# Three places of a decoder-layer kernel reordered: opening loads, the last memory values against the first `w_co` tile, and a third row buffer for the output

## The reference

```python
mk_p, mv_p = memory_kv(mem_prompt, norm_mem, w_ck, w_cv)   # rmsnorm(256 memory rows) @ w_ck, @ w_cv
h = rmsnorm(x, norm_mix);  proj = h @ w_in                 # q|k|v|z_A|alpha|beta|u|z_B
# gated DeltaNet on q, k, v, and multi-scale pooling on u, both gated
x = x + concatenate([o_a, o_b]) @ w_out
qx = rmsnorm(x, norm_cross) @ w_cq                         # 4 heads of 512
probs = softmax(qx @ mem_k / sqrt(512))                    # prompt: 256 shared memory rows
ctx = probs @ mem_v                                        # each request: its own 256 cached rows
x = x + ctx @ w_co
y = rmsnorm(x, norm_final)
```

## Time and profile before

| | us |
|---|---|
| median of 3 runs | 1631.5 (1630.23 to 1631.87) |
| the profiled execution, its time | 1630.06 |
| the profiled execution, its span | 1628.2 |
| PE busy | 1603.5 |
| DVE busy | 1019.7 |
| ACT busy | 647.7 |

### The profile page before, as it was taken

How to read it: one execution, slowest core, us unless ns; L and a number is a source line. 1 busy time by engine, 2 the same in 40 slices (tenths; PEclk the granted TensorE clock), 3 DMA queues, 4 the chain that set the end, 5 groups by cost and what they waited for, 6 DMA issues and landing times.

```text
span 1628.2 us, 31254 instructions
## 1 busy us (share of the span) xinstructions
PE 1603.5 (98%) x12618; PEld 1486.8 (91%) x12618; DVE 1019.7 (63%) x1718; ACT 647.7 (40%) x1099; POOL 184.7 (11%) x191
## 2 busy tenths in 40 slices
PE   7999999999999999999999999999999999999997
PEld 5887899999999999999999999999999996499997
DVE  5676547775856767667344563443787754399952
ACT  5666344343452444425422232222344322235442
POOL 0121000211121111211100011111000000001120
PEclk9999999999999999999999999999999999999999
DMA  7898644233242432324289956878523359953462
GB/s 271 249 302 260 217 109 116 70 94 96 76 119 53 116 96 70 101 54 130 77 197 232 247 136 183 225 217 221 145 78 104 104 224 419 369 156 106 131 187 110
DMA packets 321886, 263.35 MB, mean 162 GB/s; under 512 B 15241, under 2 KB 288530, under 8 KB 316450
## 3 DMA queue, kind: packets, MB, share of 16 engines
q1 hardware_dynamic: 299360, 245.21, 50.8%
q10 hardware_dynamic: 22434, 16.87, 3.8%
HBM read 218.09 MB, written 44.30 MB: 161 GB/s over the span
## 4 chain that ended last, share of the span: by engine, by line
PE 94%; DVE 2%; DMA 1%; ACT 1%; issue 1%; POOL 0%; DVEq 0%; SPq 0%; ACTq 0%
PE pj L288 52%; PE pj L487 11%; PE pj L2318 7%; PE dk L2318 5%; PE pj L3091 2%; PE dk L2584 2%; PE pj L2617 1%; PE dk L1907 1%; PE pj L2595 1%; PE dk L1294 1%; PE pj L2626 1%; PE dk L371 1%; PE dk L1310 1%; PE dk L1410 1%; DMA values_raw_b<-in_cache_mem_v_dram 1%
## 5 line engine op out<-in xcount | busy, mean ns | idle before, releaser
L288 PE MATMUL pj<-a_hi,w_high 128*128 128x272 f32 x1792 | 392.1, 300 | 0.0
L288 PE MATMUL pj<-a_hi,w_low 128*128 128x272 f32 x1792 | 370.2, 288 | 0.0
L288 PE MATMUL pj<-a_lo,w_high 128*128 128x272 f32 x1792 | 369.4, 288 | 0.0
L288 PEld LDWEIGHTS pj<-a_hi,w_high 128*128 128x128 f32 x1792 | 280.3, 189 | 13.0 <-issue 7.7
L288 PEld LDWEIGHTS pj<-a_lo,w_high 128*128 128x128 f32 x1792 | 281.6, 188 | 0.0
L288 PEld LDWEIGHTS pj<-a_hi,w_low 128*128 128x128 f32 x1792 | 280.0, 189 | 0.0
L272 DVE TENSOR_TENSOR w_low<-w_raw,w_high 128x2048 fp32r<-128x2048 f32 x76 | 173.6, 2284 | 94.6 <-ACT w_high L262 94.4
L262 ACT ACTIVATE w_high<-w_raw 128x2048 fp32r<-128x2048 f32 x76 | 145.6, 1915 | 83.4 <-PE pj L288 46.1
L2202 ACT ACTIVATE q_high<-q_part 128x512 fp32r<-128x512 f32 x140 | 77.5, 621 | 74.1 <-DVE q_part L2256 36.0
L288 PE MATMUL pj<-mix_hi,w_high 128*128 128x272 f32 x512 | 105.9, 288 | 0.0
L288 PE MATMUL pj<-mix_lo,w_high 128*128 128x272 f32 x512 | 105.6, 288 | 0.0
(11 more groups left out here) (477 smaller groups left out, 2933.2 us busy)
## 6 DMA issues: line engine op xcount, KB each, us to landing
w_raw<-in_w_in_dram SPq DMA_DIRECT2D x48, 1024.0 KB, 6.0
w_raw_wide<-in_w_ck_dram SPq DMA_DIRECT2D x16, 1024.0 KB, 8.9
w_raw_wide<-in_w_cv_dram SPq DMA_DIRECT2D x16, 1024.0 KB, 6.2
w_raw<-in_w_out_dram SPq DMA_DIRECT2D x16, 1024.0 KB, 7.8
q_part<-in_w_cq_dram SPq DMA_DIRECT2D x48, 256.0 KB, 3.6
w_raw<-in_w_co_dram SPq DMA_DIRECT2D x8, 1024.0 KB, 7.2
q_part<-in_w_co_dram SPq DMA_DIRECT2D x32, 256.0 KB, 3.8
kin<-in_cache_mem_k_dram ACTq DMA_DIRECT2D x18, 256.0 KB, 6.2
```

The lines of the kernel that those rows point to most:

```text
L288: mm = pe.matmul(pj[:, 2 * (q % 2) + b, 0:n], wt[:, k, :], x(k, o, n), start=(k == 0 and m == 0), stop=(k == KT - 1 and m == 2))
```

## The change

It has three parts.

1. **Opening.** SP issues the first weight tile ahead of the second block of memory rows. ACT casts that tile before it takes the second block's squares, which now come behind `take_mem(0)`. DVE's `x_scale` of the second block comes behind the remainders of turn 0. On PE `turn_mem(1)` moves into `multiply_first`, behind the 8 matmuls of m = 0.
2. **Values.** The load of the first `w_co` tile goes behind both loads of request 7's values. On ACT the cast of that tile goes behind the copy of the requests' result (`svr`).
3. **End.** Block n = 4 gets a buffer of its own, `yb_short`, in the space of the weight ring, and waits for no store.

```diff
             sp.dma_start(cst[:, 0:NFIRST], ...).then_inc(const_loaded, 16)
-            sp.dma_start(xin[1][:], t["mem_prompt"][0, P:MEM, :]).then_inc(mem1_loaded, 16)
             for q in range(3):
                 sp.dma_start(raw_wide[q][:], source("mem", 0, q)).then_inc(w_loaded[q], 16)
                 if q == 0:
+                    sp.dma_start(xin[1][:], t["mem_prompt"][0, P:MEM, :]).then_inc(mem1_loaded, 16)
...
                         pe.matmul(pj[:, m, :], x[:, k, m * P:(m + 1) * P], high_wide[0][:, k, :], ...)
+                if m == 0:
+                    turn_mem_second(pe)
                 (second, third)[m](pe)
...
             turn_mem(0)(pe)
-            turn_mem(1)(pe)
...
-            x_stats(act, 1, xin[1], P)
+            cast_high(act, "mem", 0, 0)
             act.wait_ge(vec_ready, 1)
             take_mem(0)
-            cast_high(act, "mem", 0, 0)
+            x_stats(act, 1, xin[1], P)
             take_mem(1)
...
-            x_scale(dve, 1, xin[1], P)
             take_mem(0)
+            x_scale(dve, 1, xin[1], P)
             take_mem(1)
             split_low(dve, "mem", 0, 0)
...
             load_values(sp, 6)
-            sp.dma_start(raw[0][:], source("co", 0, 0)).then_inc(w_loaded[0], 16)
             sp.wait_ge(sv_done.sem, sv_done.at(3))
             load_values(sp, 7)
+            sp.dma_start(raw[0][:], source("co", 0, 0)).then_inc(w_loaded[0], 16)
...
-                    cast_high(act, "co", 0, 0)
                     act.wait_ge(sv_done.sem, sv_done.at(8))
                     act.activation(svr[:], pj[:, 0, :], ACT.Copy).then_inc(svr_a.sem, 1)
+                    cast_high(act, "co", 0, 0)
...
+        yb_short = put("yb_short", [D], F32, M_RAW)
+        def y_buffer(n):
+            return yb_short if n == 4 else yb[n % 2]
...
-                    at_least(act, y_stored[n % 2], 16 * (n // 2))
+                    at_least(act, y_stored[n % 2], 16 if n in (2, 3) else 0)
```

More of the change, by code:

```diff
@@ L493, in multiply_mem, with multiply_first @@
                         u += 1
-        def multiply_first(pe, second, third, fourth):
+        def multiply_first(pe, turn_mem_second, second, third, fourth):
             pe.wait_ge(hi_cast, 1)
@@ L572, in pe_mem @@
                     if j == 0 and q == 0:
-                        multiply_first(pe, turn_mem(2), turn_mem(3), turn_mem(4))
+                        multiply_first(pe, turn_mem(1), turn_mem(2), turn_mem(3), turn_mem(4))
                         continue
@@ L2897, in sp_co @@
                 dst = t["y_prompt"][0, n * P:(n + 1) * P, :] if n < 4 else t["y_sample"].rearrange("b t d -> (b t) d")
-                sp.dma_start(dst, yb[n % 2][0:rows, :]).then_inc(y_stored[n % 2], 16)
+                sp.dma_start(dst, y_buffer(n)[0:rows, :]).then_inc(y_stored[n % 2], 16)
             sp.wait_ge(y_stored[0], 48)
@@ L2936, in rows_out @@
                     act.wait_ge(y_turned.sem, y_turned_at(n, c))
-                    at_least(act, y_stored[n % 2], 16 * (n // 2))
-                    act.activation(yb[n % 2][0:rows, c * 512:(c + 1) * 512], y_bank(n, c)[0:rows, :], ACT.Copy,
+                    at_least(act, y_stored[n % 2], 16 if n in (2, 3) else 0)
+                    act.activation(y_buffer(n)[0:rows, c * 512:(c + 1) * 512], y_bank(n, c)[0:rows, :], ACT.Copy,
                                    scale=rs3[0:rows, n:n + 1]).then_inc(y_act, 1)
@@ L3025, in rows_out @@
                     dve.wait_ge(y_turned.sem, y_turned_at(n, c))
-                    at_least(dve, y_stored[n % 2], 16 * (n // 2))
-                    dve.tensor_scalar(yb[n % 2][0:rows, c * 512:(c + 1) * 512], y_bank(n, c)[0:rows, :], rs3[0:rows, n:n + 1], None,
+                    at_least(dve, y_stored[n % 2], 16 if n in (2, 3) else 0)
+                    dve.tensor_scalar(y_buffer(n)[0:rows, c * 512:(c + 1) * 512], y_bank(n, c)[0:rows, :], rs3[0:rows, n:n + 1], None,
                                       ALU.mult).then_inc(y_dve.sem, 1)
```

## The result

| | before | after |
|---|---|---|
| median of 11 runs each, us | 1631.87 | 1635.04 |
| lowest and highest | 1629.26 to 1635.96 | 1633.13 to 1638.44 |
| ratio after / before | | 1.0022 [1.0013, 1.0031] |
| profiled execution: its time, its span | 1630.06, 1628.2 | 1638.44, 1636.6 |

The ratio means +3.6 us, between +2.1 and +5.1 (the medians are 3.2 apart). The changed kernel is slower, by about the amount that can just be told from no change. The prediction of 1634.2 (1630.0 to 1636.8) holds the time. The profiled execution of after is the slowest of its eleven, 3.4 above its median, so its length is not taken as the change's; it is read place by place.

What follows compares the result with a forecast made beforehand. PE was taken as the bound, busy 1603.5 of 1628.2 us, so only its idle places count. Opening +4.1, values -0.3 and end -1.1 sum to +2.7 us, giving 1634.2 (range 1630.0 to 1636.8).

Steps and rivals of the forecast that it cites:

- that is 0.9 us won: Opening: PE starts m = 0 at 13.15 instead of 14.02, with turn 0 still ending at 10.8.
- what else was moved costs nothing: Opening: SP has no wait between these loads, and other constants and the second weight tile keep their places; no cost.
- Opening, the second block: Opening: second block turned behind m = 0, DVE's splits behind its remainders; q = 1 at 27.05, not 22.93, +4.1 us.
- PE doesn't reach the higher clock before m = 1: Rival, opening: the clock rises only after q = 1 has begun, opening +6.3 us, 1636.4 in all; chance 0.16.
- The net -0.3: Values: the gain of 2.0 us to the first product of `co`, less 1.7 us lost again to the clock.
- The 1.7 for the clock: Values: the clock loss seen behind the 3.79 us wait before, taken as lost again in the first `co` tile.
- +0.2: Values: upper bound of the net, with the clock slow for somewhat longer than before.
- did no harm: Clock rival at `co`: 2.3 us idle there is nearer the 1.68 us before the last turns, which ran at full pace.
- the landing of the store: End: last store, issued 2.1 us earlier, lands 0.6 us behind block 3's, at 1626.7 instead of 1627.8, -1.1 us.
- The clock holds at `co`: Rival, values: idle time of 2.3 us leaves the clock up, values give -2.0 us, 1632.5 in all; chance 0.22.
- The second block is no later than before: Rival, opening: second block turned without holding DVE, opening -0.9 us, 1627.5 to 1629.2 in all; chance 0.10.
- m = 0 runs partly at the higher clock: Rival, opening: faster m = 0 gives +2.8 us in place of +4.1, 1632.9 in all; chance 0.10.

Runs made afterwards that it cites:

- the opening alone: Kernel before with only the change's opening part (loads and order on ACT, DVE and PE): ratio 1.0037 [1.0024, 1.0050].
- e9c: Kernel with only the opening changed, plus the `conv_w` rows' load issued first of ACT's seven small loads: ratio 1.0028 [1.0019, 1.0037] against before.
- the engines alone: Kernel before with only the opening's new order of ACT, DVE and PE, its loads as before: ratio 1.0034 [1.0022, 1.0047].
- values and end: Kernel before with the change's values and end parts, without its opening: ratio 0.9989 [0.9977, 1.0001].
- values alone: Kernel before with only the values part (first `w_co` tile's load and cast moved later): ratio 0.9995 [0.9986, 1.0004].
- the end alone: Kernel before with only the end part (block 4's own buffer `yb_short`): ratio 0.9995 [0.9987, 1.0004].

## Why the prediction was right or wrong

**The total.** Forecast +2.7, measured +3.6 (2.1 to 5.1). The three measured places give 6.2 - 0.3 - 0.7 = +5.2, taking the mean over profiles for the values, and +4.2 by the separate timings. That 5.2 lies just past the end of the interval is not explained; the profiles are single executions. Part of the agreement of the total is luck: the opening was 2.1 too small, and the time came out only 0.9 above the sum. By the prediction's own signs the opening failed, since q = 1 was to begin no later than 29 and began at 29.14 in after and 29.59 in the opening alone.

**Opening, the first product: wrong.** The step that failed is "that is 0.9 us won". It let turn 0 keep its start at 9.74. Turn 0 stands on PE behind the turn of the small rows, whose wait of 9.4 us was on the list of PE's waits before. It was read as the start of the kernel, not as a wait that a moved load can lengthen. The sentence "what else was moved costs nothing" looked at SP's queue alone. After: turn 0 at 12.21, 2.5 us later, the 0.9 lost and m = 0 at 15.90. A second, smaller miss is the landing of the first weight tile. It was given the 8.8 of the block whose place it took and landed at 9.4; in after the rows hide it, and with the rows early it costs 0.5. Why a 48 KB load on ACT's queue is late by a swap on SP's isn't shown. The weight tile comes in pieces of 2 KB and the block in pieces of 8 KB, so that there are four times as many pieces ahead, but that the number of pieces is the cause is only argued. The Trainium skill, "DMA: Bandwidth & Descriptors", section "Queues, rings and completion order", says that each DMA engine serves the queues in turn, a packet at a time; by that the rows share with whatever SP has ahead of them. No run here shows the packets in that order.

**Opening, the second block: right in DVE's chain, and 0.1 off with the rows early** (e9c: 27.15), partly because two small errors cancel. The two splits took 4.48 where 4.6 was put, back to back behind the remainders. PE's part was wrong in after and with the rows early: the forecast has it at the higher clock and standing at the fifth turn. There the pace of the matmuls rose about the end of m = 0 and fell again in m = 1, which took 3.31 and 2.81 instead of 1.83, and PE worked without a stop until q = 1, ending within 0.1 of DVE. In the opening and the engines alone it ran at the full pace and waited 1.5 for DVE at that turn, and q = 1 came at 29.6 and 29.8. So the loss does not need the slow clock. The rival "PE doesn't reach the higher clock before m = 1" gave nearly the measured opening, +6.3, and its sign, eight matmuls of m = 1 over 3 us, came true in after, but for a reason that isn't the cause: it put 29.2 on a slow PE, and with PE fast it was 29.59.

**Values: right in the path.** Forecast -2.0 to the first product of `co`, measured -2.2 in after and in values and end, -1.6 in values alone; a new wait of 2.3 to 3.2, measured 2.9 and 3.0. The tile landed 27.6 us behind V, as forecast (1419.5 less 1391.87). The net -0.3 is met by the mean over profiles, -0.3, but that this fits so closely is chance, with three profiles 2.1 apart; the timing of values alone gives -0.8 (-2.3 to +0.7). The 1.7 for the clock was the middle, but the clock is no fixed term: 0, 1.7 and 3.4 in three profiles of the same order. The bound "+0.2" was too near, after itself being at +0.5. The argument from the 1.68 us at the end, which "did no harm", doesn't stand: behind that same wait the turns were slow in five of fourteen profiles. The rule cited in the prediction from the Trainium skill ("TensorE: Matmul & The Clock Gate", "HAM oscillation — how this bites in real kernels") agrees in nine of the eleven profiles with a long wait here, and in two it doesn't.

**End: direction right, size smaller.** Forecast -1.1, measured -0.7 in after and in values and end. The term mis-sized is the landing of the store, put at 0.6 behind that of block 3. In after, block 3's store was issued at 1630.46 and landed 4.8 later, the last one at 1632.19 and 4.0 later, 0.9 behind it. And the whole term holds only if the 20 turns run at the full pace: in the end alone it was 0.

**Rivals.** "The clock holds at `co`" is what values alone shows, and not by the length of the wait, which was nearly the same (2.9 against 3.0); what decides it is not shown. "The second block is no later than before" fell with every profile of the opening, and so did "m = 0 runs partly at the higher clock": its eight matmuls took 3.5 to 3.8 us in each.

## What to carry to other kernels

Of a list of waits, the first row of an engine is a wait too: a small load that everything stands behind can be moved by the order of large loads on another queue, and belongs at the head of its own. A reorder of loads that already run at the full rate of the DMA engines moved a stall here and hardly shortened it (3.8 us became 3.0 to 3.8), so follow what the last of them feeds before counting a gain. Where a stall can't be taken out, look at what it does to the clock behind it: four unneeded matmuls in it won 1.6 us here (0.2 to 3.3), about as much as values and end together (1.8, -0.2 to 3.8), though the intervals are wide and three in the other wait showed no gain in the timing.

## What the runs showed of the hardware

- The order of a 1 MB load in 2 KB pieces and one in 8 KB pieces on SP's queue moved the landing of small rows on ACT's queue from 9.3-10.1 to 11.2-12.1 us (nine and four profiles).
- After a like wait of 2.9 to 3.9 us in attention the clock cost 0, 1.7 or 3.4 us (two, seven and two of eleven profiles), differing between kernels that are the same at that place; it did not fall behind a wait there that was filled with matmuls (three profiles). Ahead of the last turns it fell around a wait of 1.7 us in five of fourteen.
- The granted clock of the records stands at 1.00 from 12 to 20 us of the opening in before and after, while the matmuls of m = 0 go at half the pace of m = 1. There it is the duration of the matmuls, not the granted clock, that tells the pace.
- A 256 KB store took 2.6 us to land when issued 3.9 us behind one of 1 MB (before), and 4.0 us when issued 1.7 us behind it (after).
